# Head loop of a hybrid GDN, S5 and cross-attention block in a new order: unnormalized q and k, earlier convolutions, masks first on Pool, transposes in the triangular inverse

## Chip, cores and metric

One core of one Trainium2 chip. The metric is device time in microseconds, the median of the runs; lower is better. TensorE does the matmuls, VectorE the elementwise work, ACT the activations, Pool (GpSimd) elementwise work and some transfers, SP the weight loads.

## The reference, cut to what matters

One layer on x of 512 x 2048 in float32. x is normalized and multiplied by w_in; the columns of the product feed three branches and their gates. The branch of this case is the gated delta rule, 8 heads of 128:

```python
qkv = jax.nn.silu(causal_depthwise_conv(qkv_raw, conv_w))
q = l2norm(q) * (GDN_HEAD_DIM ** -0.5)
k = l2norm(k)
...
lower = jnp.where(strict, jnp.einsum('bnhid,bnhjd->bnhij', k_beta, k) * decay, 0.0)
sol = lax.linalg.triangular_solve(eye + lower, rhs, left_side=True, lower=True, unit_diagonal=True)
...
v_new = u_n - jnp.einsum('bhcd,bhde->bhce', w_n, state)
o = jnp.einsum('bhcd,bhde->bhce', qd_n, state) + jnp.einsum('bhij,bhje->bhie', qk_n, v_new)
...
o = rmsnorm(o, out_norm_g)
```

l2norm divides by the root of a row's sum of squares plus 1e-6, rmsnorm by the root of the mean of squares plus 1e-6. A second branch, S5, is a complex linear recurrence in groups; a third is attention to a memory. At the end the gated branches are multiplied by their weights, summed and multiplied by w_out.

## The kernel before, in words

The program runs in phases that all engines leave together: set-up, attention, the head loop (mixer), the S5 gate product, the branch products and the output product. Large products are made of float32 numbers split in a high part of reduced precision (ACT, `split_hi`, L402) and the rest (VectorE, `split_lo`, L411), with three matmuls of 512 columns for each tile (`mm3`, L420). Two weight buffers alternate: a block's load into raw waits until TensorE has used the block two before (`load_halves`, L370).

**The head loop.** In a trip (`mixer`) TensorE computes ten blocks of 128 columns of the input projection for head a: q, k, v, a gate, z_b, a gate, z_a, two gates, x_b. Each block is eight eighths of six matmuls, so a trip has 80 eighths. Between them stands the small work of two older heads: j = a - 1 goes through norms, decays, the triangular inverse and the S5 inputs, l = a - 2 through its recurrence over four chunks of 128, its output norm and the store. `until(e)` on TensorE issues big matmuls up to eighth e; what stands after it runs next. An eighth waits for its half of the block's wl, and the first one also until ACT has emptied the PSUM bank. The order of every engine is written by hand, and each works strictly in order; semaphores are waited for where a value or a buffer is needed. Ten trips are run, mixers 0 to 9: 0 has blocks only, 1 has no l, 2 to 8 are full, 9 has l and two blocks.

**The order of before.** On VectorE (`mixer`, L1706), split(b) makes the low half of block b + 1. After split(0) come the states of the recurrence, the three convolutions of j (`convolve`, L1577) and the S5 matrices; after split(1) the S5 states of group 0 (`s5_states`, L1678: six products from PSUM, then two scans) and the gated output of l (`gated`, L1669: reciprocal, gain, z); after split(2) the decays' differences and the scaling of k and q (L1603, L1609); after split(3) `keys`, `system`, `values`; then the first level of the inverse (`first_level`, L1639) and six levels (`level_x`, `level_p`). `keys` (L1619) writes kbg, and kbg also holds the gated output of l until it is stored: the wait on g_st at L1625 is for that store, which Pool issues in `store_head` (L612).

On ACT (`mixer`, L1287), end_of(b) empties block b (`tile_out`) and splits block b + 2. The split of block 1 stands first, then the negated weights (`weights_out`), new values, SiLU and squares of q, k and v, the S5 tables (`s5_tables`, sine and cosine) and roots.

On Pool (`mixer`, L553) stand the arguments of the S5 tables for group 0, the S5 store, arguments(1), turn_back(0) (the S5 states turned back by the tables), the head's store, the masks (strict and upper triangle, times beta), and the rest.

**The inverse.** It is built by doubling: tl holds it, tu its transpose. A level multiplies the transposed lower matrix by tl (`level_x`, L843), VectorE masks the product to gx, and TensorE forms two products, tu with gx for the change of tl and gx with tu for that of tu (`level_p`, L855, L861 and L862). A float32 product of 128 columns is two passes in the profile; a transpose is one.

## Time and profile before

| | us |
|---|---|
| median of 3 runs | 2438.35 |
| lowest, highest | 2429.41, 2440.11 |
| profiled execution, its own time | 2434.2 |
| its span | 2432.6 |
| VectorE busy | 1272.6 |
| ACT busy | 816.4 |
| Pool busy | 718.8 |

The span runs from the first to the last instruction of the profiled execution. A busy share is a mean over stages that have different limits. Matmul rows overlap, so the distance between two starts tells what one costs, not its duration.

### The profile page before, as it was taken

What the parts mean: (1) busy time and instruction counts of PE and PEld (TensorE: products, weight loads), DVE (VectorE), ACT (ScalarE), POOL (GpSimd) and SP (SyncE); (2) the same over time, 40 slices, a digit from 0 to 9 for tenths busy, and PEclk for the clock granted to TensorE, in tenths of its full rate; (3) what the DMA queues carried; (4) which work ended last, traced back from release to release, by engine and by line L of the source; (5) the groups of instructions that cost most, each with busy time, mean ns of one, the idle gap of its engine ahead of it and who ended that gap; (6) DMA issues with size and microseconds to landing.
All of it is one profiled execution on the core that took longest, in us unless ns stands there. A gap on an engine that the chain in (4) does not pass through costs nothing.

```text
span 2432.6 us, 29926 instructions
## 1 busy us (share of the span) xinstructions
PE 2292.5 (94%) x10744; PEld 1816.8 (75%) x10744; DVE 1272.6 (52%) x1495; ACT 816.4 (34%) x1042; POOL 718.8 (30%) x554
## 2 busy tenths in 40 slices
PE   4999999999999999999999999999999989999996
PEld 3888876877767777677777776776777877877885
DVE  4433332286495584864955848648523334445233
ACT  5433321353252432422524324325224222123221
POOL 0000000066284372642843726627310100000000
PEclk9999998999999999999999999999999999999998
DMA  4444432422322222222322322232235545554343
GB/s 159 122 122 121 115 101 70 122 79 75 87 80 81 65 81 75 69 78 80 83 76 72 82 75 69 78 84 80 77 91 160 174 137 166 156 162 147 115 129 111
DMA packets 374343, 249.74 MB, mean 103 GB/s; under 512 B 21305, under 2 KB 349186, under 8 KB 372738
## 3 DMA queue, kind: packets, MB, share of 16 engines
q1 hardware_dynamic: 355954, 193.21, 29.1%
q0 software_dynamic: 11408, 43.00, 5.3%
q10 hardware_dynamic: 6912, 12.59, 1.4%
q8 instruction: 47, 0.77, 0.1%
q14 instruction: 22, 0.18, 0.0%
HBM read 221.50 MB, written 27.26 MB: 102 GB/s over the span
## 4 chain that ended last, share of the span: by engine, by line
PE 79%; DVE 9%; DMA 5%; ACT 4%; issue 2%; SPq 0%; DVEq 0%; POOLq 0%; ACTq 0%; POOL 0%
PE bank L422 22%; PE bank L424 22%; PE bank L423 21%; DMA raw<-in_w_in_dram 4%; DVE wl L416 2%; PE bank L862 2%; PE bank L861 2%; PE bank L852 2%; PE bank L919 1%; PE bank L926 1%; ACT wh L408 1%; PE bank L927 1%; PE bank L920 1%; DVE rk L1605 1%; DVE tl L1671 1%
## 5 line engine op out<-in xcount | busy, mean ns | idle before, releaser
L416 DVE TENSOR_TENSOR wl<-raw,wh 128x1024 fp32r<-128x1024 f32 x352 | 474.5, 1359 | 605.6 <-ACT wh L408 605.1
L422 PE MATMUL bank<-uh,wh 128*128 128x512 f32 (+1 forms) x1808 | 747.6, 414 | 15.7 <-DVE wl L416 10.9
L423 PE MATMUL bank<-ul,wh 128*128 128x512 f32 (+1 forms) x1808 | 709.1, 392 | 0.0
L424 PE MATMUL bank<-uh,wl 128*128 128x512 f32 x1792 | 706.2, 394 | 0.0
L408 ACT ACTIVATE wh<-raw 128x1024 fp32r<-128x1024 f32 x352 | 370.5, 1057 | 700.5 <-DMA raw<-in_w_in_dram 306.2
L422 PEld LDWEIGHTS bank<-uh,wh 128*128 128x128 f32 (+1 forms) x1808 | 341.4, 189 | 139.6 <-issue 61.6
L424 PEld LDWEIGHTS bank<-uh,wl 128*128 128x128 f32 x1792 | 339.0, 189 | 75.7
L423 PEld LDWEIGHTS bank<-ul,wh 128*128 128x128 f32 (+1 forms) x1808 | 341.9, 189 | 69.5 <-issue 6.5
L422 PE MATMUL bank<-gh,wh 128*128 128x512 f32 x512 | 202.6, 396 | 12.2 <-DVE gl L1774 12.2
L424 PE MATMUL bank<-gh,wl 128*128 128x512 f32 x512 | 200.9, 392 | 0.0
L423 PE MATMUL bank<-gl,wh 128*128 128x512 f32 x512 | 200.2, 391 | 0.0
L565 POOL TENSOR_SCALAR karg<-cst,s5h 128x512 f32<-128x512 f32 x32 | 39.7, 1241 | 346.8 <-DVE hph L1555 219.4
L1206 ACT ACTIVATE gk<-bank 128x512 f32<-128x512 f32 x48 | 28.7, 597 | 277.6 <-PE bank L424 277.4
L422 PEld LDWEIGHTS bank<-gh,wh 128*128 128x128 f32 x512 | 96.7, 189 | 33.4 <-issue 11.4
L585 POOL TENSOR_TENSOR hr<-tcos,gr 128x512 f32<-128x512 f32 x32 | 48.6, 1520 | 247.2 <-PE bank L927 189.6
L542 POOL DMA_DIRECT2D gated_c<-ox x8 | 4.5, 565 | 369.9 <-DVE ox L1466 369.4
L424 PEld LDWEIGHTS bank<-gh,wl 128*128 128x128 f32 x512 | 96.5, 189 | 22.4
L423 PEld LDWEIGHTS bank<-gl,wh 128*128 128x128 f32 x512 | 96.7, 189 | 21.0
L422 PE MATMUL bank<-wh,uh 128*128 128x512 f32 x256 | 100.2, 391 | 3.2 <-DVE ul L1803 3.2
L424 PE MATMUL bank<-wh,ul 128*128 128x512 f32 x256 | 100.3, 392 | 0.0
L423 PE MATMUL bank<-wl,uh 128*128 128x512 f32 x256 | 100.3, 392 | 0.0
L672 POOL DMA_DIRECT2D gates<-gates x24 | 17.1, 713 | 237.0 <-DVE merged L1791 148.1
(301 smaller groups left out, 3257.6 us busy)
## 6 DMA issues: line engine op xcount, KB each, us to landing
raw<-in_w_in_dram SPq DMA_DIRECT2D x224, 512.0 KB, 3.9
raw<-in_w_kv_mem_dram SPq DMA_DIRECT2D x32, 512.0 KB, 3.9
raw<-in_w_out_dram SPq DMA_DIRECT2D x32, 512.0 KB, 3.9
gates<-gk ACTq DMA_DIRECT2D x48, 256.0 KB, 4.4
gates<-gates POOLq DMA_DIRECT2D x24, 512.0 KB, 4.6
raw<-in_s_w_glu_dram SPq DMA_DIRECT2D x16, 512.0 KB, 3.8
raw<-in_w_br_c_dram SPq DMA_DIRECT2D x16, 512.0 KB, 3.8
raw<-in_w_br_a_dram SPq DMA_DIRECT2D x16, 512.0 KB, 3.8
```

Source lines behind the costliest of these rows:

```text
L408: act.activation(k.wh[slot][:, c], k.raw[slot][:, c], ACT.Copy).then_inc(k.w_hi, 1)
L416: dve.tensor_tensor(k.wl[slot][:, c], k.raw[slot][:, c], k.wh[slot][:, c].bitcast(F32), ALU.subtract).then_inc(k.w_lo, 1)
L422: pe.matmul(o, ah, bh, start=start, stop=False)
L423: pe.matmul(o, ah, bl, start=False, stop=False)
L424: return pe.matmul(o, al, bh, start=False, stop=stop)
L565: ts(k.karg[:, :], k.tvec, hi_, ROUND, ALU.mult, ALU.add).then_inc(k.args, 1)
L585: pool.tensor_tensor(o[:, :], c1[:, :], a[:, :], ALU.mult).then_inc(k.dem, 1)
L852: mm = pe.matmul(ps[2][:, n * P:(n + 1) * P], k.lt[:, n, :], k.tl[:, n, :], start=True, stop=True)
L861: pe.matmul(ps[6][:, c], k.tu[:, n, :], k.gx[:, n, :], start=True, stop=True)
L862: mm = pe.matmul(ps[7][:, c], k.gx[:, n, :], k.tu[:, n, :], start=True, stop=True)
L919: pe.matmul(ps[3][:, :], k.bc[r, 0, :], k.xb[r, :], start=True, stop=True)
L1206: act.activation(k.gk[n][:, :], o[:, :], ACT.Sigmoid).then_inc(k.mx_out, 1)
```

## The change

The keys and queries are not normalized any more. The squares of k are summed in columns (`norm_keys`: the squares as weights, one column of ones), which gives one number for each row; its reciprocal, times beta and decays, is folded into small tiles (`key_scales`, hk) that scale the masks, kbg and the values. The query's norm is folded into the output norm: the squares of q, scaled by the constant of the norm, are added to the sum of squares of the output in the same bank. The convolutions and SiLU of head a are done in the trip that projects them, near its end. On Pool the masks and decayed queries come before the head's store and before arguments(1). In levels 1 to 5 the second product goes; tl is updated first and its transpose, by four TensorE transposes, is copied to tu. `level_x` now waits for tl alone. The weights product of l comes before the trip's first eighth, the S5 output of group 3 right after it, and most small work of j stands at other eighths. ACT does the negated weights before the split of block 1, and the S5 tables of group 1 before end_of(2). The functions left out below have only their waits and scale tiles changed to match.

```diff
-        if j: arguments(1); turn_back(0)
+        if j: masks(); decayed_queries()
         if l: store_head()
-        if j: masks(); arguments(2); decayed_queries(); turn_back(1); arguments(3); turn_back(2); turn_back(3)
+        if j: arguments(1); turn_back(0); arguments(2); turn_back(1); arguments(3); turn_back(2); turn_back(3)
...
     def norm_keys(j):
-        pe.wait_ge(k.sq, count(j, 2, 2))
-        wait(pe, k.oroot, count(j, 0, 1))
-        pe.matmul(ps[6][:, :], ones, k.rk[:, :], start=True, stop=True).then_inc(k.ss, 1)
+        pe.wait_ge(k.sq, count(j, 1, 2))
+        for n in range(NT):
+            mm = pe.matmul(ps[6][:, n:n + 1], k.rk[:, n * P:(n + 1) * P], ones[:, 0:1], start=True, stop=True)
+        mm.then_inc(k.ss, 1)
         pe.wait_ge(k.gu, count(j, 1, 1))
         wait(pe, k.st_s, count(j, 0, 3))
         pe.matmul(ps[7][:, :], ones, k.gx[:, :, :], start=True, stop=True).then_inc(k.rsum, 1)
...
     def keys(j):
-        pe.wait_ge(k.qk, count(j, 1, 2))
+        pe.wait_ge(k.silu, count(j, 2, 3))
+        pe.wait_ge(k.rn, count(j, 1, 4))
+        wait(pe, k.oroot, count(j, 0, 1))
...
+    def level_t(j, l):
+        pe.wait_ge(k.tus, count(j, 2 * l - 1, 11))
+        for n in range(NT):
+            mm = pe.transpose(ps[7][:, n * P:(n + 1) * P], k.tl[:, n, :], ident)
+        mm.then_inc(k.ltt, 1)
...
-    def output_norm(j):
+    def output_norm(j, nxt):
         pe.wait_ge(k.osq, count(j, 1, 1))
-        pe.matmul(ps[6][:, :], ones, k.lt[:, :, :], start=True, stop=True).then_inc(k.sso, 1)
+        pe.wait_ge(k.sq, count(j, 2, 2))
+        if nxt:
+            pe.wait_ge(k.rn, count(nxt, 1, 4))
+        pe.matmul(ps[6][:, :], ones, k.lt[:, :, :], start=True, stop=False)
+        pe.matmul(ps[6][:, :], ones, k.rq[:, :], start=False, stop=True).then_inc(k.sso, 1)
...
+        if l: weights(l)
         until(1)
-        if l: weights(l)
+        if l: s5_outputs(l, 3)
...
         if l: chunk_output(l, 3)
-        until(11)
-        if l: output_norm(l)
+        until(10)
+        if j: norm_keys(j)
         until(13)
+        if l: output_norm(l, j)
+        until(15)
         if j: s5_matrices(j)
-        until(15)
+        until(18)
         if j: s5_inputs(j, 0)
-        until(17)
-        if j: norm_keys(j)
-        until(25)
-        if j: norm_queries(j)
+        until(20)
+        if j: keys(j)
+        until(21)
+        if j: keys_keys(j)
+        until(26)
+        if j: values(j)
         until(29)
-        if j: keys(j); keys_keys(j); s5_inputs(j, 1)
+        if j: turn_lower(j)
         until(31)
-        if j: values(j); s5_outputs(j, 0)
+        if j: keys_queries(j)
         until(33)
-        if j: turn_lower(j)
+        if j: s5_inputs(j, 1)
         until(36)
-        if j: keys_queries(j)
+        if j: s5_outputs(j, 0)
+        until(38)
+        if j: level_x(j, 1)
+        until(41)
+        if j: level_p(j, 1)
+        until(43)
+        if j: level_t(j, 1)
         until(45)
-        if j: level_x(j, 1); s5_inputs(j, 2)
+        if j: level_x(j, 2); s5_inputs(j, 2)
         until(48)
-        if j: level_p(j, 1)
-        until(51)
-        if j: level_x(j, 2)
+        if j: level_p(j, 2)
+        until(50)
+        if j: level_t(j, 2)
         until(52)
-        if j: s5_outputs(j, 1)
-        until(54)
-        if j: level_p(j, 2)
+        if j: level_x(j, 3); s5_outputs(j, 1)
+        until(55)
+        if j: level_p(j, 3)
         until(57)
-        if j: level_x(j, 3)
+        if j: level_t(j, 3)
+        until(58)
+        if j: level_x(j, 4)
         until(60)
-        if j: level_p(j, 3); s5_inputs(j, 3)
+        if j: s5_inputs(j, 3)
+        until(61)
+        if j: level_p(j, 4)
         until(63)
-        if j: level_x(j, 4)
-        until(66)
-        if j: level_p(j, 4)
+        if j: level_t(j, 4)
+        until(65)
+        if j: level_x(j, 5)
         until(67)
         if j: s5_outputs(j, 2)
         until(69)
-        if j: level_x(j, 5)
-        until(72)
         if j: level_p(j, 5)
-        until(75)
+        until(71)
+        if j: level_t(j, 5)
+        until(74)
         if j: level_x(j, 6)
-        until(78)
+        until(77)
...
+        if l: weights_out(l)
         split_hi(k, act, B_MIX + 1, PER, a)
-        if l: weights_out(l); new_values(l, 0); new_values(l, 1); new_values(l, 2)
+        if l: new_values(l, 0); new_values(l, 1)
         if j: tile_out(j, M_XB)
-        if l: new_values(l, 3)
-        if j: activation_of(j, 0)
+        if l: new_values(l, 2); new_values(l, 3); output_squares(l)
         end_of(0)
-        if l: output_squares(l)
-        if j: s5_matrices(j); activation_of(j, 1); activation_of(j, 2); s5_tables(j, 0)
+        if j: row_decays(j); decays(j)
         if l: output_root(l)
+        if j: key_root(j); s5_matrices(j); s5_tables(j, 0); query_squares(j)
         end_of(1)
-        if j: key_root(j); s5_tables(j, 1)
         if blocks > 2:
+            if j: s5_tables(j, 1)
             end_of(2)
-            if j: query_root(j); decays(j); keep_z(j)
+            if j: keep_z(j); lower_turned(j)
             end_of(3)
-            if j: lower_turned(j)
             end_of(4)
             if j: s5_tables(j, 2)
             end_of(5)
             end_of(6)
             if j: s5_tables(j, 3)
             end_of(7)
+            if gate is None: activation_of(a, 0)
             end_of(8)
+            if gate is None: activation_of(a, 1); activation_of(a, 2); key_squares(a)
...
+    def key_scales(j):
+        dve.wait_ge(k.ss, count(j, 1, 1))
+        ts(k.hk[:, 0, :], ps[6][:, 0:NT], EPS, None, ALU.add).then_inc(k.rn, 1)
+        dve.wait_ge(k.rn, count(j, 1, 4))
+        dve.reciprocal(k.hk[:, 0, :], k.hk[:, 0, :]).then_inc(k.rn, 1)
+        dve.wait_ge(k.rn, count(j, 2, 4))
+        tt(k.hk[:, 1, :], k.hk[:, 0, :], k.hph[:, 2, :], ALU.mult).then_inc(k.rn, 1)
+        tt(k.hk[:, 2, :], k.hk[:, 0, :], k.hph[:, 0, :], ALU.mult).then_inc(k.rn, 1)
...
         wait(dve, k.g_st, count(j, 0, 16))
-        tt(k.kbg[:, :, :], chunked(ps[6][:, :]), rows(k.hph[:, 2, :]), ALU.mult).then_inc(k.kb, 1)
+        dve.wait_ge(k.rn, count(j, 3, 4))
+        tt(k.kbg[:, :, :], chunked(ps[6][:, :]), rows(k.hk[:, 1, :]), ALU.mult).then_inc(k.kb, 1)
...
+    def level_t(j, l):
+        dve.wait_ge(k.ltt, count(j, l, 5))
+        dve.tensor_copy(k.tu[:, :, :], chunked(ps[7][:, :])).then_inc(k.tus, 1)
...
         split(0)
         if l: state(l, 0)
         if j: head_parameters(j)
-        if l: state(l, 1); s5_sum(l)
+        if l: s5_sum(l)
         if j: log_decays(j)
+        if l: state(l, 1)
         if l: state(l, 2)
-        if j: convolve(j, 0); s5_matrices(j); convolve(j, 1); convolve(j, 2)
+        if j: s5_matrices(j); key_scales(j); differences(j)
         split(1)
         if j: s5_states(j, 0, 0); s5_states(j, 0, 1)
         if l: gated(l)
+        if j: keys(j); system(j)
         split(2)
-        if j: differences(j); normed_keys(j)
-        if j: normed_queries(j)
+        if j: values(j); first_level(j); queries(j)
         split(3)
-        if j: keys(j); system(j); values(j); s5_states(j, 1, 0); s5_states(j, 1, 1)
+        if j: s5_states(j, 1, 0); s5_states(j, 1, 1)
         split(4)
-        if j: first_level(j); queries(j)
+        if j: level_x(j, 1); level_p(j, 1); level_t(j, 1)
+        if j: s5_states(j, 2, 0)
         split(5)
-        if j: level_x(j, 1); s5_states(j, 2, 0); level_p(j, 1)
+        if j: level_x(j, 2); s5_states(j, 2, 1); level_p(j, 2); level_t(j, 2)
+        if heads: conv_weights(a); convolve(a, 0)
         split(6)
-        if j: s5_states(j, 2, 1); level_x(j, 2); level_p(j, 2)
+        if j: level_x(j, 3); level_p(j, 3); level_t(j, 3); level_x(j, 4)
         split(7)
-        if j: level_x(j, 3); level_p(j, 3); s5_states(j, 3, 0); level_x(j, 4); s5_states(j, 3, 1)
+        if j: s5_states(j, 3, 0); level_p(j, 4); s5_states(j, 3, 1); level_t(j, 4)
+        if heads: convolve(a, 1)
         split(8)
-        if j: level_p(j, 4); level_x(j, 5); level_p(j, 5)
+        if j: level_x(j, 5)
+        if heads: convolve(a, 2)
+        if j: level_p(j, 5); level_t(j, 5)
         split(9)
         if j: level_x(j, 6); level_p(j, 6)
```

## Rows read from the trace of the kernel before

**Rows 1.** The page: span, then TensorE's busy time, share of span and instructions.
```profile
span 2432.6 us, 29926 instructions
...
PE 2292.5 (94%) x10744; PEld 1816.8 (75%) x10744; DVE 1272.6 (52%) x1495; ACT 816.4 (34%) x1042; POOL 718.8 (30%) x554
```

**Rows 2.** Windows: trips (mixers 1 and 5), then 3.4 us; PEclk is granted clock.
```profile
489.40:636.30 146.90, 146.07 (x683) 113.35 (x682) 105.97 (x115) 55.46 (x66) 84.89 (x57) 1.00 0.31 82
...
1124.67:1287.50 162.83, 156.63 (x731) 119.82 (x730) 107.77 (x122) 57.94 (x73) 85.71 (x59) 0.99 0.28 76
...
1130.60:1134.00 3.40, 3.40 (x10) 2.82 (x11) 0.64 (x1) 0.28 (x1) 0.00 (x0) 0.50 0.00 0
```

**Rows 3.** Waits of TensorE: who waited for whom, us in total, times, longest.
```profile
PE bank L880 <- ACT dl L1272: 17.7, 8, 3.3
...
PE bank L901 <- ACT lt L1280: 11.7, 8, 3.3
...
PE bank L817 <- DVE kc L1607: 9.9, 7, 2.2
...
PE bank L861 <- DVE gx L1653: 6.8, 8, 2.5
```

**Rows 4.** Timeline of TensorE in one trip: start, us, what, idle before.
```profile
1163.71 1.02 PE L798 MATMUL bank<-rk,cst 128*128 128x512 f32 x2
1164.56 1.02 PE L801 MATMUL bank<-gx,cst 128*128 128x512 f32 x2
...
1173.40 0.39 PE L424 MATMUL bank<-uh,wl 128*128 128x512 f32 x1
...
1174.76 0.39 PE L424 MATMUL bank<-uh,wl 128*128 128x512 f32 x1
1176.44 0.50 PE L422 MATMUL bank<-uh,wh 128*128 128x512 f32 x1 [1.30 <-DVE wl L416]
...
1197.08 0.60 PE L840 MATMUL bank<-cst,dl 128*128 128x128 f32 x4
1197.43 0.48 PE L422 MATMUL bank<-uh,wh 128*128 128x512 f32 x1
...
1222.18 0.38 PE L861 MATMUL bank<-gx,tu 128*128 128x128 f32 x2
...
1223.88 0.48 PE L422 MATMUL bank<-uh,wh 128*128 128x512 f32 x1
```

**Rows 5.** Timeline of VectorE in the same trip.
```profile
1130.01 1.23 DVE L416 TENSOR_TENSOR wl<-raw,wh 128x1024 fp32r<-128x1024 f32 x1 [5.11 <-ACT wh L408]
...
1161.15 0.69 DVE L1692 TENSOR_TENSOR ma<-bank,tcos 128x512 f32<-128x512 f32 x1 [3.35 <-PE bank L920]
...
1165.25 2.19 DVE L1699 TENSOR_TENSOR_SCAN gr<-s5h,gr 128x512 f32<-128x512 f32 x1
...
1168.93 3.32 DVE L1671 RECIPROCAL tl<-lt 128x512 f32<-128x512 f32 x1
...
1174.08 4.54 DVE L416 TENSOR_TENSOR wl<-raw,wh 128x1024 fp32r<-128x1024 f32 x2
...
1192.23 0.68 DVE L1626 TENSOR_TENSOR kbg<-bank,hph 128x512 f32<-128x512 f32 x1
...
1194.03 0.68 DVE L1617 TENSOR_TENSOR vb<-bank,hph 128x512 f32<-128x512 f32 x1
...
1209.04 1.78 DVE L1645 TENSOR_TENSOR tu<-lt,cst 128x512 f32<-128x512 f32 x1
...
1231.27 1.22 DVE L1699 TENSOR_TENSOR_SCAN gr<-s5h,gr 128x512 f32<-128x512 f32 x1
...
1233.53 0.67 DVE L1653 TENSOR_TENSOR gx<-bank,cst 128x512 f32<-128x512 f32 x1
```

**Rows 6.** Timeline of Pool, its store; then the transfer's size and us to landing.
```profile
1182.07 0.62 POOL L614 DMA_DIRECT2D gated_a<-kbg  x1 [0.83 <-POOL hi L588]
...
gated_a<-kbg POOLq DMA_DIRECT2D x1, 256.0 KB, 2.4
```

More of the change, by code:

```diff
@@ L51 @@
 C_COL = C_T + S
-COLS = ["eps", "eps128", "quarter", "even", "odd", "neven", "nodd"]
+COLS = ["eps", "epssq", "quarter", "even", "odd", "neven", "nodd"]
 NCONST = C_COL + len(COLS)
@@ L561, in arguments @@
             if q == 0:
-                wait_apart(k, pool, k.sliced, count(j, 3, 3))
+                wait_apart(k, pool, k.sliced, count(j, 2, 2))
             wait_apart(k, pool, k.tab, count(j, 3 * q, 12))
@@ L801, in norm_keys @@
         pe.matmul(ps[7][:, :], ones, k.gx[:, :, :], start=True, stop=True).then_inc(k.rsum, 1)
-    def norm_queries(j):
-        wait(pe, k.og, count(j, 0, 2))
-        pe.matmul(ps[2][:, :], ones, k.rq[:, :], start=True, stop=True).then_inc(k.ss, 1)
     def values(j):
         pe.wait_ge(k.silu, count(j, 3, 3))
-        pe.wait_ge(k.root, count(j, 2, 2))
+        wait(pe, k.og, count(j, 0, 2))
         for n in range(NT):
@@ L828, in keys_queries @@
     def keys_queries(j):
-        pe.wait_ge(k.qk, count(j, 2, 2))
+        pe.wait_ge(k.silu, count(j, 1, 3))
         pe.wait_ge(k.vb_s, count(j, 1, 1))
@@ L857, in level_p @@
         pe.wait_ge(k.xm, count(j, l, 6))
+        if l == 1:
+            pe.wait_ge(k.tu_s, count(j, 4, 4))
+        else:
+            pe.wait_ge(k.tus, count(j, 2 * (l - 1), 11))
         for n in range(NT):
@@ L860, in level_p @@
             if l < 6:
[L861 to L862 removed]
+                mm = pe.matmul(ps[6][:, c], k.tu[:, n, :], k.gx[:, n, :], start=True, stop=True)
+            else:
+                mm = pe.matmul(ps[7][:, c], k.gx[:, n, :], k.tu[:, n, :], start=True, stop=True)
         mm.then_inc(k.lp, 1)
+    def level_t(j, l):
[3 more added lines that the diff above has]
+        mm.then_inc(k.ltt, 1)
     def weights(j):
@@ L1583, in convolve @@
         wait(dve, k.vtr, count(j, 0, 1))
+        wait(dve, k.sq, count(j, 0, 2))
+        wait(dve, k.pm, count(j, 0, 4))
         ts(dst[:, :], src[:, 0:S], k.cwh[:, 0, part:part + 1], None, ALU.mult).then_inc(k.conv, 1)
```

80 lines of the change are left out of this document (41 added, 39 removed).

## The prediction

> **What bounds the kernel now.** I read the page first. TensorE works in 94% of the span [rows 1], so time comes off in two ways only: fewer matrix passes, or shorter holes between them. VectorE, at 52%, matters where TensorE stands waiting for it. The profiled execution took 2434.2 us, 1.6 more than its span; the median of the three runs is 4 us higher. The windows by trip come second: a full trip of the head loop takes 162.8 us, of which TensorE is idle 6.2 [rows 2]. Seven trips are full (blocks, head work and recurrence together, mixers 2 to 8); the one before has head work but no recurrence, the last has recurrence alone. Third, the waits of TensorE name the holes [rows 3]: 17.7 us in 8 trips at the first new value, 11.7 at the output norm, 9.9 at the transposes of k, 6.8 at a level. A sixth hole, 1.3 us, stands before block 3 in one timeline [rows 4]. After the hole at the new values TensorE runs 3.4 us at a granted clock of 0.50, which is 1.2 GHz instead of 2.4 [rows 2].
>
> I count time as eighths of a block. Six matmuls of 512 columns lie between 1173.40 and 1174.76, so an eighth is 1.36 us [rows 4]. From that and the passes between them I can say when TensorE comes to each block, and from VectorE's timeline when that block's low half is ready.
>
> **What the change takes away, per full trip.**
> - The negated weights no longer stand behind a split that waits for its transfer: 17.7/8 = 2.2 us, and most of the slow clock behind it (3.4 us at half speed is 1.7; I take 1.2, as not every trip need have it).
> - Squares of the output right behind the last value: 11.7/8 = 1.5. k isn't scaled any more: 9.9/7 = 1.4. The level's hole: 0.9. The old hole before block 3: 1.3.
> - Passes. A level's two products take 1.70 us from 1222.18 to 1223.88 [rows 4], so one takes 0.85. Its replacement, four transposes, is a row of 0.60 including the tail of its pipeline [rows 4]; 0.45 with the step back to the big matmuls. That is 0.4 saved, five times: 2.0. The k norm took 0.85 (1163.71 to 1164.56 [rows 4]); eight passes of one column are not in the trace and cost between nothing and 0.85 (the eight of a level product); I take 0.45, saving 0.4. The q norm only moves into the output norm: 0. Both reciprocals of 512 columns and two products leave VectorE, with no gain by themselves; the convolutions move to the end of the trip, where VectorE has waits of several us between levels, also 0, and if that cover were gone they'd cost 3 us each. One ACT table switch more or less lies beside TensorE: 0.
>
> Together 8.5 + 2.4 = 10.9 us.
>
> **What it adds.** Here I walk VectorE's queue, because it is strictly in order.
>
> Block 3. VectorE's list was: S5 states of group 0, gated output, split of block 3, and keys much later. It becomes: states, gated output, *keys, system*, split of block 3. `keys` overwrites kbg, which the gated output has just filled and Pool stores to memory, so L1625 waits for that store to land. Before, some 18 us lay between; now nothing does. From the start of the states: products 4.1 (1161.15 to 1165.25), the two scans 3.7 with Pool at work or, as Pool will then be idle, 2.3 (1231.27 to 1233.53), reciprocal and gating 5.15 less 0.35 for the same reason [rows 5]; Pool's wake-up and issue 0.7 and 2.4 to landing [rows 6]; three products at 0.6 (1192.23 to 1194.03), so 1.8; first half of the split 2.3 (half of 4.54) as Pool has started its arguments again, or 1.2 if it does not collide [rows 5]. Sum 18.4, or 17.3. TensorE's side: before, from 1161.15 to the end of the big matmul that starts 1174.76 are 13.8 us [rows 4, 5]: nine eighths and the norm. Now the S5 inputs come at eighth 18 instead of 15, so six eighths, 8.2, and the twelve passes of keys and k-by-k at 0.106 each, 1.3, less the start-up of 0.1: 9.4. TensorE stands **9.0 us** (7.9 without the collision). Behind a hole of 2.2 on average it fell to half clock [rows 2, 3], so I add 1.5. Behind the waiting keys in VectorE's queue stand the split, the values and the first level.
>
> Block 4. The split of block 4 now stands behind `first_level` and `queries`. From the transposes of the lower matrix: copy 0.8, three VectorE operations of 1.78 (L1645) [rows 5], queries 0.6, first half of the split 2.3 = 8.8. TensorE has three eighths and the eight k-by-q passes, 5.0. Hole **3.8**. The 1.78 are with Pool busy, and Pool, whose arguments and turn-back of group 0 were all pushed behind the store, is busy then. Were it idle they'd take about 0.62 (half of 1.23 for 1024 columns) and the split 1.2: no hole. So 0 to 3.8; I take 3.8, the nearest rows being the same operations. ACT's copy of that matrix now stands behind the tables of group 1, and these behind Pool's arguments, later by the store; I find it ready about when the transposes are, and count nothing.
>
> Level 2. The S5 inputs of group 2 come at eighth 45, level 2's second product at 48, three eighths = 4.1 later. VectorE needs 0.3 + 2.05 (three products), the whole split of block 6 (4.54, or 2.46 alone) and the mask 0.7: 7.6 or 5.5. Hole 1.4 to 3.5, taken 3.3 (arguments of group 3 run beside it). Then VectorE does the second part of the states, 2.05 + 2.3, and 0.7 for the difference, before the transposes can go: 5.2 against 3.6 of TensorE: **1.6**. A second fall of the clock behind these, half likely: 0.8.
>
> From there to the end of the trip I find every split ready at least 1 us early, the last level by 0.6 only.
>
> Added: 9.0 + 1.5 + 3.8 + 3.3 + 1.6 + 0.8 = 20.0. Net **+9.1 per full trip, +64** for seven. The trip without recurrence has no store and no gating: block 3 costs only 1, so 1 + 3.8 + 3.3 + 1.6 + 0.8 - 3.2 (0.8 of its holes and the 2.4 of passes) = +7. The last trip gains its two holes and clock and pays two more passes: -4. With the profiled 2434.2 that is 2501; I say **2500**, and as the median stands 4 above that execution the error from this is small.
>
> **A rule that speaks against the transposes.** In the trace the four transposes of L840 are followed by big matmuls at the usual pace, and the clock does not fall there [rows 2, 4]. The Trainium skill, TensorE: Matmul & The Clock Gate, Part 4 (PE-mode transpose), says that transposes do not count as TensorE activity for the clock gate the way products do. By it five more such groups per trip could let the clock fall; the trace does not bear this out for four passes between long products.
>
> **Rivals.**
> - *Clock falls at the transposes.* Five groups, up to 1.7 us each: 8.5 a trip, 68 in all: 2568. Against it the row of L840. 3%.
> - *The holes close* (the other side). The store's landing, the collisions and the level order don't reach TensorE, because VectorE comes to its splits earlier than I walk. All of the 10.9 stays: 2434 - 76 - 3 - 4 = 2351. It decides where the new holes together fall under 10.9 us a trip. For it: VectorE loses 8 us of work a trip. Against it: block 3's 7.9 alone needs no collision. 9%, with its milder forms 12%.
> - *Even.* Pool and VectorE never collide and the clock stays up: 7.9 + 0 + 0 + 1.4 + 1.6 = 10.9 against 10.9: about 2434, with one clock fall 2445. The walk's errors of a microsecond a trip put it either side. 12%.
> - *The tail too.* With Pool's work later, the last level (0.6 us early) and the convolutions before it come late as well, 2 to 3 us a trip: 2518. 15%, inside the range.
> - *The change does not do what it says*: the masks are first on Pool but wait for the decays, which need TensorE's sum at eighth 10, so Pool idles in front of them; that is in my walk and needs no case.
>
> **Numbers.** My case (net +4 to +13 a trip, 2460 to 2530) has 58%, the tail 15%, the clock rival 3%, even 12%, holes closed 12%. About 0.5% (12 us) can be told from no change: the even case gives 11 of its 12 to the middle and one to faster, so faster 0.13, same 0.11, slower 0.76. The range goes from the even case, 2430, to all costs high (the store landing 2 us later, a third fall of the clock: +14 a trip), 2535.
>
> **What would show it.** Right: TensorE's longest waits are for the split wl, about 9 us once a trip before block 3, VectorE idle 3 us before kbg on a transfer named gated, then 3 to 4 us before block 4; granted clock under 1 behind them; no wait left at the new values; about 2.4 us less TensorE work per trip. Wrong: if VectorE's wait before kbg is under 1 us, the term of the store falls; if TensorE arrives at block 3 later than 47 us into the trip, my count of passes is off; if the wait before block 4 is missing, the collision was.

## The result, and the profile after

The kernel after takes **2499.43 us** (median of 4 runs, 2498.14 to 2501.73); the kernel before took 2438.90 in the runs beside it. The ratio is **1.0268**, 95% interval 1.0246 to 1.0290: slower by 60.5 us. The forecast was 2500. One execution of the nine of experiment 4 took 4625.43 us and stands in no ratio.

The page of the profiled execution after, the span and the line of busy times:

```profile
span 2499.7 us, 29937 instructions
...
PE 2306.1 (92%) x10632; PEld 1815.2 (73%) x10632; DVE 1177.0 (47%) x1503; ACT 801.4 (32%) x1032; POOL 701.2 (28%) x554
```

Beside [rows 1] VectorE has 96 us less to do, ACT 15 and Pool 18, and TensorE issues 112 matmuls fewer. Yet TensorE's busy time is 14 us *longer*, and the span 67: fewer passes took more time, which points to the clock; the rest of the 67 is holes, less what the passes gave back.

Windows of the kernel after: the trips of mixers 1 and 3, then 3.4 us behind its first hole (us; busy time of PE, PEld, DVE, ACT, POOL; granted clock, DMA share, GB/s):

```profile
489.30:640.90 151.60, 145.08 (x676) 111.20 (x674) 90.74 (x115) 52.99 (x64) 83.23 (x57) 1.00 0.30 79
815.56:988.60 173.04, 159.67 (x719) 120.15 (x718) 95.18 (x122) 56.37 (x72) 81.65 (x59) 0.94 0.27 72
870.00:873.40 3.40, 3.39 (x8) 2.72 (x9) 2.24 (x2) 0.00 (x0) 3.19 (x2) 0.50 0.00 0
```

A full trip took 162.8 us with a granted clock of 0.99 [rows 2]; now it takes 173.0 with 0.94. The seven full trips are 169.6 to 176.2 us long, together 60.5 us more than before, and mixer 1 is 4.7 longer.

TensorE's waits, and two of VectorE's, in the kernel after (total us, times, longest):

```profile
PE bank L425 <- DVE wl L419: 77.8, 16, 8.7
DVE tu L1694 <- ACT lt L1309: 32.7, 8, 5.0
DVE kbg L1675 <- DMA gated_a<-kbg: 22.0, 7, 3.4
PE bank L869 <- DVE gx L1702: 17.4, 8, 2.7
PE bank L878 <- DVE tl L1707: 13.3, 13, 2.1
```

All four lines of [rows 3] are gone. In their place TensorE waits for the low half of a block's weights (wl), in 7 trips twice, and at levels 2 and 5 of the inverse.

TensorE's timeline in one trip after (start, us, what, idle before):

```profile
835.37 0.95 PE L803 MATMUL bank<-cst,rk 128*128 128x1 f32 x8
836.18 1.10 PE L807 MATMUL bank<-gx,cst 128*128 128x512 f32 x2
...
870.01 0.79 PE L425 MATMUL bank<-uh,wh 128*128 128x512 f32 x1 [7.87 <-DVE wl L419]
...
887.52 0.50 PE L425 MATMUL bank<-uh,wh 128*128 128x512 f32 x1 [2.42 <-DVE wl L419]
...
925.33 1.15 PE L869 MATMUL bank<-gx,tu 128*128 128x128 f32 x8 [1.32 <-DVE gx L1702]
...
930.13 0.66 PE L878 MATMUL bank<-cst,tl 128*128 128x128 f32 x4 [0.91 <-DVE tl L1707]
930.54 0.47 PE L425 MATMUL bank<-uh,wh 128*128 128x512 f32 x1
```

VectorE's timeline in the same trip:

```profile
852.65 0.69 DVE L1746 TENSOR_TENSOR ma<-bank,tcos 128x512 f32<-128x512 f32 x1 [9.74 <-PE bank L940]
...
859.01 3.33 DVE L1725 RECIPROCAL tl<-lt 128x512 f32<-128x512 f32 x1
...
863.16 0.69 DVE L1730 TENSOR_TENSOR kbg<-kbg,zk 128x512 f32<-128x512 f32 x1
866.93 0.69 DVE L1675 TENSOR_TENSOR kbg<-bank,hk 128x512 f32<-128x512 f32 x1 [3.09 <-DMA gated_a<-kbg]
...
868.74 3.43 DVE L419 TENSOR_TENSOR wl<-raw,wh 128x1024 fp32r<-128x1024 f32 x2
...
881.40 0.95 DVE L1694 TENSOR_TENSOR tu<-lt,cst 128x512 f32<-128x512 f32 x1 [3.69 <-ACT lt L1309]
882.27 1.76 DVE L1696 TENSOR_TENSOR tl<-cst,tl 128x512 f32<-128x512 f32 x1
883.96 1.78 DVE L1698 TENSOR_TENSOR tu<-cst,tu 128x512 f32<-128x512 f32 x1
```

Read these two side by side and the chain of the first hole stands there: states, reciprocal, gating, the store (3.09 us of waiting in front of kbg), three products, half a split, TensorE. From 852.65 to 870.01 are 17.36 us. The prediction's walk gave 18.4, or 17.3 without the collision. Note also the first row: VectorE is **idle for 9.7 us in front of this chain**.

Pool and ACT in the same trip after, and the store's transfer (256 KB, us to landing):

```profile
864.51 0.58 POOL L619 DMA_DIRECT2D gated_a<-kbg  x1 [16.65 <-DVE kbg L1730]
...
875.27 0.62 POOL L579 TENSOR_SCALAR farg<-farg 128x512 f32<-128x512 f32 x1 [0.20 <-POOL farg L577]
```

```profile
876.07 0.63 ACT L1258 ACTIVATE tsin<-farg 128x512 f32<-128x512 f32 x1 [23.00 <-POOL farg L579]
...
880.78 0.59 ACT L1309 ACTIVATE lt<-bank 128x512 f32<-128x512 f32 x1
```

```profile
gated_a<-kbg POOLq DMA_DIRECT2D x8, 256.0 KB, 2.4
```

Here is a second chain, of which the prediction counted nothing: the same gated output, the store, Pool's seven operations of arguments(1) (to 875.9), ACT's tables, and only behind them ACT's copy of the lower matrix, which VectorE needs for the first level and, behind that, for the split of block 4.

**The account per full trip**, by adding up the idle stretches between TensorE's matmuls over the seven trips. What is lost to the clock is an estimate: half of TensorE's busy time at 1.2 GHz.

| us per trip | before | after | predicted after |
|---|---|---|---|
| hole at block 3 | 1.3 | 8.0 | 9.0 |
| hole at block 4 | 0 | 2.3 | 3.8 |
| level 2, product and transposes | 0 | 2.2 + 0.8 | 3.3 + 1.6 |
| level 5, transposes | 0 | 0.7 | 0 |
| other holes | 5.9 | 0.1 | 0 |
| lost to the clock | 1.7 | 6.1 | 2.8 |

Holes +6.8, clock +4.4 (before rounding 4.35); the trips grew by 60.5/7 = 8.6, so the passes gave 2.5 back (predicted 2.4). (The 2.8 is 2.3 added and the 0.5 that the prediction left of the old 1.7.)

### The profile page after: what moved, and what is told of

Same layout as the page of the kernel before. It is cut to its first block and busy times, and to the rows that moved or that the text cites. A ratio compares the mean times of both kernels' runs of the same rounds, so it can differ in the third digit from the quotient of the medians.

```text
span 2499.7 us, 29937 instructions
## 1 busy us (share of the span) xinstructions
PE 2306.1 (92%) x10632; PEld 1815.2 (73%) x10632; DVE 1177.0 (47%) x1503; ACT 801.4 (32%) x1032; POOL 701.2 (28%) x554
## 5 line engine op out<-in xcount | busy, mean ns | idle before, releaser
L425 PE MATMUL bank<-uh,wh 128*128 128x512 f32 (+1 forms) x1808 | 762.0, 421 | 82.7 <-DVE wl L419 77.8
L419 DVE TENSOR_TENSOR wl<-raw,wh 128x1024 fp32r<-128x1024 f32 x352 | 448.0, 1288 | 598.4 <-ACT wh L411 597.3
L426 PE MATMUL bank<-ul,wh 128*128 128x512 f32 (+1 forms) x1808 | 718.5, 397 | 0.0
L427 PE MATMUL bank<-uh,wl 128*128 128x512 f32 x1792 | 715.0, 399 | 0.0
L425 PEld LDWEIGHTS bank<-uh,wh 128*128 128x128 f32 (+1 forms) x1808 | 346.9, 192 | 211.0 <-DVE wl L419 74.3
L427 PEld LDWEIGHTS bank<-uh,wl 128*128 128x128 f32 x1792 | 344.3, 192 | 79.0
L426 PEld LDWEIGHTS bank<-ul,wh 128*128 128x128 f32 (+1 forms) x1808 | 347.9, 192 | 67.1 <-issue 4.5
L1746 DVE TENSOR_TENSOR ma<-bank,tcos 128x512 f32<-128x512 f32 x64 | 44.1, 689 | 158.0 <-PE bank L940 142.5
L426 PEld LDWEIGHTS bank<-gl,wh 128*128 128x128 f32 x512 | 97.2, 190 | 21.5
L568 POOL TENSOR_SCALAR karg<-cst,s5h 128x512 f32<-128x512 f32 x32 | 24.6, 768 | 237.7 <-DVE hph L1596 202.4
```

The source lines that it names most:

```text
L419: dve.tensor_tensor(k.wl[slot][:, c], k.raw[slot][:, c], k.wh[slot][:, c].bitcast(F32), ALU.subtract).then_inc(k.w_lo, 1)
L425: pe.matmul(o, ah, bh, start=start, stop=False)
L426: pe.matmul(o, ah, bl, start=False, stop=False)
L427: return pe.matmul(o, al, bh, start=False, stop=stop)
L568: ts(k.karg[:, :], k.tvec, hi_, ROUND, ALU.mult, ALU.add).then_inc(k.args, 1)
L1746: tt(k.ma[:, :], x1[:, :], c[:, :], ALU.mult).then_inc(k.mod, 1)
```

## The experiments

Unless said otherwise each is the kernel after with one edit. But for 7, 8 and 10 TensorE's order stays that of the kernel after, so holes can be compared by place. Where ranges per trip are given without more, they are those of mixers 2 to 7.

**1. The split in front of the whole chain.**

```diff
         split(1)
+        split(2)
         if j: s5_states(j, 0, 0); s5_states(j, 0, 1)
         if l: gated(l)
         if j: keys(j); system(j)
-        split(2)
```

> The changed kernel with one move on VectorE: the split of block 3 stands before the S5 states of group 0 and the gated output, instead of behind keys and system. The hole of 7.9 us before block 3 must go in every theory. Theory A (one chain: gated output, store, Pool's arguments of group 1, ACT's tables of group 1, copy of the lower matrix, first level, split of block 4): the split pushes that whole chain 2 to 3 us later, so block 4 begins at 74 to 75 us of the trip instead of 72.0; the hole before block 4 grows from 2.3 to some 14 us and the time is 2500 to 2520. Rival B (the hole before block 3 is a cost of its own): 7.9 us and up to 3 us of slow clock come off each of seven trips, the hole before block 4 stays near 2.3, and the time is 2425 to 2445.

Measured 2506.88 us, ratio 1.0299 (1.0264 to 1.0333): A, with a smaller hole than its 14. The hole at block 3 is gone in every trip; one of 11.2 us stands before block 4 (10.1 in mixer 8), one of 0.9 before the values. The clock loses 1.5 to 5.8 in mixers 2 to 7, in stretches of up to 20.5 us. Two waits of this kernel:

```profile
PE bank L425 <- DVE wl L419: 83.1, 9, 11.2
DVE tu L1694 <- ACT lt L1309: 69.5, 8, 10.9
```

So the hole is no property of block 3: it is a debt that the next block pays. The second line says what it waits for: VectorE stands 8.7 us a trip before the first level, until ACT's copy is there; in the kernel after it was 4.1.

**2. The store from a tile of its own**, so that nothing waits for its landing before the last level.

```diff
-                           k.kbg[:, :, :].rearrange("p n c -> p (n c)")).then_inc(k.g_st, 16)
+                           k.gout[:, :, :].rearrange("p n c -> p (n c)")).then_inc(k.g_st, 16)
...
-        wait(dve, k.g_st, count(j, 0, 16))
...
         tt(k.kbg[:, :, :], chunked(ps[6][:, :]), rows(k.hk[:, 1, :]), ALU.mult).then_inc(k.kb, 1)
...
-        stt(k.kbg[:, :, :], chunked(ps[2][:, :]), k.prm2[:, 104:105], k.tl[:, :, :], ALU.mult, ALU.mult)
+        stt(k.gout[:, :, :], chunked(ps[2][:, :]), k.prm2[:, 104:105], k.tl[:, :, :], ALU.mult, ALU.mult)
...
-        if j: level_x(j, 6); level_p(j, 6)
+        if j: wait(dve, k.g_st, count(j, 0, 16)); level_x(j, 6); level_p(j, 6)
```

> The changed kernel with a buffer of its own for the gated output, so that keys does not wait for the store. In both theories the wait before kbg (3.1 us) goes and the hole before block 3 falls from 7.9 to 4.8 us. Theory A: Pool issues the store and its arguments at the same moment as before, so block 4 still begins at 71 to 72 us of the trip and its hole grows to about 5; time 2490 to 2500. Rival B (the store wait costs what it takes): 3.1 us in each of seven trips and a little slow clock, 2470 to 2478.

Measured 2512.57, ratio 1.0308 (1.0275 to 1.0341). A's mechanism, above both ranges: the hole at block 3 falls by the 3.1 us of the store to 4.85, the one at block 4 grows from 2.3 to between 5.0 and 6.7 in mixers 2 to 7, and the clock loses 3.5 to 11.7 a trip. The holes' sum hardly changed (13.6 for 14.0); the time went up. Its window of a trip (mixer 4):

```profile
995.00:1170.90 175.90, 162.44 (x719) 122.55 (x718) 94.37 (x122) 56.37 (x72) 79.51 (x59) 0.93 0.26 71
```

**3. Pool's arguments in front of the store.**

```diff
-        if j: masks(); decayed_queries()
+        if j: masks(); decayed_queries(); arguments(1)
         if l: store_head()
-        if j: arguments(1); turn_back(0); arguments(2); turn_back(1); arguments(3); turn_back(2); turn_back(3)
+        if j: turn_back(0); arguments(2); turn_back(1); arguments(3); turn_back(2); turn_back(3)
```

> The changed kernel with Pool's arguments of group 1 before the store of the head, in the 16 us in which Pool waits for the gated output. Theory A says the Pool part of the chain goes, but the transposes of the lower matrix, which wait for keys, are ready at nearly the same moment (80.1 against 80.8 on one clock), so alone it brings little: hole before block 3 stays 7.9, the copy of the lower matrix comes 0.5 us earlier, time 2485 to 2500. Rival C (Pool's late arguments are the main fault): block 4's hole and the later ones close, 2455 to 2475.

Measured 2472.67, ratio 1.0147 (1.0116 to 1.0178): in C's range, well under A's. The hole at block 3 stays (8.4; 9.1 in mixer 8), that at block 4 falls to 0.5 in most trips (1.5 at most), and the clock loses 2.4 to 3.6 in the full trips. C's "and the later ones close" isn't borne out: those at levels 2 and 5 stay, 1.3 to 2.6, 0.9 and 0.8. VectorE at the first level in this kernel, and Pool beside it:

```profile
876.49 0.69 DVE L1694 TENSOR_TENSOR tu<-lt,cst 128x512 f32<-128x512 f32 x1 [4.03 <-ACT lt L1309]
877.10 0.69 DVE L1696 TENSOR_TENSOR tl<-cst,tl 128x512 f32<-128x512 f32 x1
877.70 1.77 DVE L1698 TENSOR_TENSOR tu<-cst,tu 128x512 f32<-128x512 f32 x1
```

```profile
875.70 1.57 POOL L575 TENSOR_SCALAR karg<-cst,s5h 128x512 f32<-128x512 f32 x1 [0.21 <-POOL farg L573]
877.45 1.47 POOL L577 TENSOR_TENSOR farg<-farg,karg 128x512 f32<-128x512 f32 x1 [0.18 <-POOL karg L575]
```

Two of the three take 0.69 instead of 0.95 and 1.76. Pool isn't idle beside them, it is at arguments(2); what changed is the kind of its operation. The two that are quick begin beside a TENSOR_SCALAR, the slow third beside a TENSOR_TENSOR, and in the kernel after all three stand beside TENSOR_TENSORs of turn_back(0) (880.50 to 885.18). ACT's copy waits for TensorE's transposes (97.2 us in 8 trips) and no longer for Pool.

**4. All repairs that I then believed in, together**: 2 and 3, the split of block 3 before the gated output, that of block 4 before the values, ACT's tables(1) behind end_of(2), level 2 reordered, and the last convolution behind level 5; that of q stayed in front of level 3.

> All together: own buffer for the gated output, Pool's arguments before the store, the split of block 3 before the gated output, the split of block 4 before the values, ACT's end of block 2 before the tables of group 1, the split of block 6 and the mask of level 2 before the S5 states of group 2, the last convolution behind level 5. Theory A: with the chain cut at each link TensorE has under 1 us of holes in a trip and no slow clock, a trip takes 151 to 153 us, and the whole 2350 to 2370, well under the kernel before (2439). Rival B adds up the single terms and comes to the same here, so it is the three others that tell them apart. If the passes saved are less than I counted (2.4 us a trip), the trip stays at 154 and the time at 2375.

Measured 2449.43, ratio 1.0067 (1.0050 to 1.0084): 80 us above the range, a miss. Waits and VectorE's timeline of this kernel:

```profile
PE bank L870 <- DVE gx L1701: 44.2, 7, 6.4
...
PE bank L814 <- DVE gout L1729: 21.9, 7, 3.2
```

```profile
1081.33 5.05 DVE L1634 SCALAR_TENSOR_TENSOR qc<-qraw,cwh,qc 128x512 f32<-128x512 f32 x3
1086.30 4.48 DVE L420 TENSOR_TENSOR wl<-raw,wh 128x1024 fp32r<-128x1024 f32 x2
1090.70 0.68 DVE L1701 TENSOR_TENSOR gx<-bank,cst 128x512 f32<-128x512 f32 x1
```

Two new holes with one cause each. The values' bank is free only once the gated output has been read from it, and that now stood behind a split: 3.2 us. And in front of gx of level 3 stood a convolution (5.05, where the same three took 2.33 in a trip of the kernel after) and a split of 4.48: 6.4 us. In mixer 8, which has no next head to convolve, the 6.4 is missing and the trip takes 158.4 instead of 167.3. So both orders have to be walked to the end of the trip.

**5. One line moved: the gated output in front of the states**, into VectorE's 9.7 idle us.

```diff
         split(1)
+        if l: gated(l)
         if j: s5_states(j, 0, 0); s5_states(j, 0, 1)
-        if l: gated(l)
         if j: keys(j); system(j)
```

> The changed kernel with one move on VectorE: the gated output of l stands before the S5 states of group 0, in the 9.7 us in which VectorE waits for the S5 products. Theory A (one chain through the gated output and its store): reciprocal and gating fit in that wait, the store is out by 34 us of the trip and keys finds it landed, Pool's arguments follow at once. The first half of the split of block 3 ends at 46.6 to 47.8 us against 46.3 wanted: hole 0.5 to 1.5 instead of 7.9, little slow clock; block 4 keeps a hole of 1 to 4 us since first level and queries still stand before its split. Trip 158 to 162 us, time 2400 to 2435. Rival B (sum of the single terms: only the store's 3 us and the 5 of the gating leave): the same hole but all that follows unchanged, 2440 to 2450.

Measured **2398.65**, ratio 0.9843 (0.9817 to 0.9868), just under A's range. VectorE in this kernel:

```profile
985.60 3.35 DVE L1725 RECIPROCAL tl<-lt 128x512 f32<-128x512 f32 x1 [0.98 <-ACT lt L1325]
...
989.78 0.69 DVE L1730 TENSOR_TENSOR kbg<-kbg,zk 128x512 f32<-128x512 f32 x1
994.37 0.69 DVE L1746 TENSOR_TENSOR ma<-bank,tcos 128x512 f32<-128x512 f32 x1 [3.90 <-PE bank L940]
...
1001.04 0.66 DVE L1675 TENSOR_TENSOR kbg<-bank,hk 128x512 f32<-128x512 f32 x1
```

The reciprocal and gating fill the idle time, the store lands under the states, kbg waits for nothing. Holes at block 3 and 4 are 0.3 and 0.5 (1.3 and 0.6 in mixer 8), trips 157.9 to 158.9 us, and the clock loses at most 1.7. The holes of level 2 (2.5, and 0.9 in most) and level 5 (0.8) stay. Both chains begin at this one operation, so one move shortens both.

**6. That, and the rest of the chains cut**: split of block 3 before keys, of block 4 before the first level, ACT's tables(1) behind end_of(2), the mask of level 2 before the states of group 2, convolutions behind the levels that TensorE waits for.

```diff
-        if j: keys(j); system(j)
         split(2)
-        if j: values(j); first_level(j); queries(j)
+        if j: keys(j); system(j); values(j)
         split(3)
+        if j: first_level(j); queries(j)
...
-        if j: s5_states(j, 2, 0)
...
-        if j: level_x(j, 2); s5_states(j, 2, 1); level_p(j, 2); level_t(j, 2)
-        if heads: conv_weights(a); convolve(a, 0)
+        if j: level_x(j, 2); s5_states(j, 2, 0); level_p(j, 2); s5_states(j, 2, 1); level_t(j, 2)
         split(6)
-        if j: level_x(j, 3); level_p(j, 3); level_t(j, 3); level_x(j, 4)
+        if j: level_x(j, 3)
+        if heads: conv_weights(a); convolve(a, 0)
+        if j: level_p(j, 3); level_t(j, 3); level_x(j, 4)
...
```

> The kernel of the run before with the other links cut: the split of block 3 before keys, the split of block 4 before the first level, ACT's end of block 2 before the tables of group 1, the split of block 6 and the mask of level 2 before the S5 states of group 2, the second part of these behind level 2's difference, the convolution of q behind the mask of level 3 and that of v behind level 5. Theory A: no hole over 1 us in a full trip, no slow clock, trip 151 to 153.5, time 2350 to 2372. If a queue has again a hidden wait, one hole of 2 to 6 us shows at one place in every trip and the time is 2375 to 2430.

Measured **2345.48**, ratio 0.9628 (0.9603 to 0.9652): the fastest kernel here, 90.5 us under before in the runs beside it (2435.99), and under A's range by 5. A trip of it:

```profile
936.30:1087.90 151.60, 151.60 (x719) 116.53 (x718) 99.91 (x122) 56.64 (x72) 84.69 (x59) 1.00 0.30 82
```

TensorE's busy time equals the window: no hole in any full trip but one of 0.4, the clock never under 1.00. So 151.6 is what the passes cost by themselves. Mixers 2 to 7 of before took 162.6 in the mean; less 6.5 of holes, 1.1 of clock and 2.4 of passes that is 152.6. The kernel after gives the same, 152.4, without its holes and clock, so the last 0.8 goes with the holes as well (TensorE's start behind each would do it; this wasn't measured by itself).

**7. The same with two products per level**, as before, in place of product and transposes.

```diff
-                mm = pe.matmul(ps[6][:, c], k.tu[:, n, :], k.gx[:, n, :], start=True, stop=True)
-            else:
-                mm = pe.matmul(ps[7][:, c], k.gx[:, n, :], k.tu[:, n, :], start=True, stop=True)
+                pe.matmul(ps[6][:, c], k.tu[:, n, :], k.gx[:, n, :], start=True, stop=True)
+            mm = pe.matmul(ps[7][:, c], k.gx[:, n, :], k.tu[:, n, :], start=True, stop=True)
...
```

> The kernel of the run before with the two products of each level as in the kernel before, and without the transposes. By my count a level then costs TensorE 0.4 us more, 2.0 a trip, 16 us over eight trips: 16 to 18 us over the run before. Rival (the transposes lower the clock or cost a start-up of their own): difference 0 or below.

Measured 2366.36, ratio 0.9709 (0.9685 to 0.9733): 20.9 over experiment 6, 3 more than expected. A trip takes 3.2 us more, 0.9 of it a hole at the last level that wasn't expected; the other 2.3 are five levels at 0.46. The transposes give about what was predicted (0.4), and no full trip loses anything to the clock with them or without.

**8. The gain by itself**: the kernel before, with only ACT's negated weights moved in front of the split of block 1.

```diff
+        if l: weights_out(l)
         split_hi(k, act, B_MIX + 1, PER, a)
-        if l: weights_out(l); new_values(l, 0); new_values(l, 1); new_values(l, 2)
+        if l: new_values(l, 0); new_values(l, 1); new_values(l, 2)
```

> The kernel before with one move on ACT: the negated weights stand before the split of block 1. The hole at the first new value (2.1 us) and the slow clock behind it (1.7 us in five of seven trips, 2.9 in the last) must go: 8 holes of 2.2 and 11 us of clock, 28 us, so 2405 to 2415. Rival: the later split of block 1 opens a hole of its own before block 1, and the gain is under 10 us.

Measured 2410.84, ratio 0.9901 (0.9871 to 0.9931). The wait of [rows 3] at the new values is gone and with it the slow clock of mixers 2 to 7: trips 159.1 to 160.1, 3.0 us less in the mean. The prediction had 2.2 + 1.2. Mixer 8 gains nothing (171.8 for 171.4): its hole at the new values is gone, but it loses 8.1 to the clock where it lost 5.1.

**9. The split of block 3 in front of keys** (after the gated output).

```diff
-        if j: keys(j); system(j)
         split(2)
-        if j: values(j); first_level(j); queries(j)
+        if j: keys(j); system(j); values(j); first_level(j); queries(j)
```

> After, with one edit: the split of block 3 stands in front of keys and system in VectorE's queue, so it no longer waits for the store of the gated output. Theory A (the store wait is one half of a chain, and work pushed behind the split meets the next hole): the hole at block 3 falls from 7.9 to about 3.3 us (3.1 of wait and 1.8 of products no longer in front), but the keys, values and first level come later by the split's own time where the store has landed meanwhile, so the hole before block 4 stays at 2 to 3.5, and the clock behind the holes gives back some: trip 167 to 171, total 2462 to 2485. Theory B (the hole only moves, as when the split stood in front of the states): hole at block 4 over 6 us, total 2490 to 2510.

Measured 2503.90, ratio 1.0277 (1.0257 to 1.0298): B. The hole at block 3 falls to 2.9, but that before block 4 is 7.0 to 8.7. VectorE, then ACT, in this kernel:

```profile
1037.03 0.68 DVE L1692 TENSOR_TENSOR tl<-dl,cst 128x512 f32<-128x512 f32 x1
1048.43 1.66 DVE L1694 TENSOR_TENSOR tu<-lt,cst 128x512 f32<-128x512 f32 x1 [10.72 <-ACT lt L1309]
```

```profile
1043.12 0.63 ACT L1258 ACTIVATE tsin<-farg 128x512 f32<-128x512 f32 x1 [22.65 <-POOL farg L579]
...
1047.82 0.58 ACT L1309 ACTIVATE lt<-bank 128x512 f32<-128x512 f32 x1
```

VectorE idles 10.7 us in front of the first level. Theory A looked at VectorE's queue alone; in this kernel the hole is made by ACT's queue.

**10. The S5 inputs of group 0 two eighths sooner**: `until(18)` before them becomes `until(16)`.

> After, with one number changed: TensorE issues the S5 inputs of group 0 at eighth 16 instead of 18. VectorE stands idle 9.7 us in front of the states, so the whole chain (states, gating, store, keys, split, values, first level) starts 2.7 us sooner while TensorE's arrival at block 3 stays. Theory A (start of the states sets the block 3 hole): hole 7.9 falls to about 5.2, hole before block 4 unchanged as both sides of it shift with the hole, total 2470 to 2485 with some of the clock. Theory B (something else, the store's landing or Pool, sets it): block 3 hole within 1 us of 7.9, total 2492 to 2505.

Measured 2470.76, ratio 1.0133 (1.0114 to 1.0152): A's time with B's hole. The states start 2.2 us sooner (for the tables now, and not for TensorE), but block 3's hole shrinks only from 7.9 to 7.1; block 4's goes from 2.3 to 1.3 in the mean of the full trips, which neither theory had. VectorE and the store's transfer:

```profile
1012.07 0.69 DVE L1746 TENSOR_TENSOR ma<-bank,tcos 128x512 f32<-128x512 f32 x1 [7.50 <-ACT tcos L1261]
...
1027.81 0.69 DVE L1675 TENSOR_TENSOR kbg<-bank,hk 128x512 f32<-128x512 f32 x1 [4.54 <-DMA gated_a<-kbg]
```

```profile
gated_a<-kbg POOLq DMA_DIRECT2D x8, 256.0 KB, 3.7
```

The store now takes 3.7 us to land instead of 2.4, and eats 1.4 of the 2.2. Per full trip 1.6 us of holes and 2.5 of clock went, which for seven trips is the 29 us. The trace names what runs beside the store: in mixers 2 to 7 the next weight load (SP, 512 KB) begins 1.2 us after the store's issue, and 177 to 226 KB of it move between the store's first packet and its last; in the kernel after it was 7 KB at most. The store's first packet comes at 2.1 to 2.2 us instead of 1.2. Where the load begins later, in mixer 8 (2.0 us), the store lands in 2.6. No run moved the load alone.

**11. Experiment 9, and ACT's tables(1) behind the copy of the lower matrix.**

```diff
-            if j: s5_tables(j, 1)
             end_of(2)
-            if j: keep_z(j); lower_turned(j)
+            if j: keep_z(j); lower_turned(j); s5_tables(j, 1)
```

> The kernel with the split of block 3 before keys, and one more edit: ACT makes the S5 tables of group 1 behind its copy of the lower matrix instead of in front of it. Theory A (the hole that moved to block 4 is ACT's: store, Pool's arguments(1), 10.3 us, the tables, and only then the copy, 7.4 us after TensorE's transposes are done): the copy starts within 1 us of the transposes, VectorE's wait of 10.7 us for it falls to about 3, the hole before block 4 falls from 8.6 to between 0 and 3 (by whether its three operations take 0.68 or 1.7 with Pool busy), trip 163 to 167, total 2440 to 2462. Theory B (VectorE or Pool would be late anyway): hole at block 4 still over 5 us, total over 2485.

Measured 2469.31, ratio 1.0116 (1.0053 to 1.0180). In this kernel:

```profile
1033.81 1.35 DVE L1693 TENSOR_TENSOR tu<-lt,cst 128x512 f32<-128x512 f32 x1 [3.61 <-ACT lt L1309]
```

The hole before block 4 falls from 7.0 to 8.7 to between 2.1 and 3.2, VectorE's wait from 10.7 to 3.6, and 35 us of time go with it: the second chain runs through ACT's queue, and A's mechanism holds. The total is 7 us above A's range, as the clock took more and not less: 6.6 a full trip for 5.4, in spite of 5.6 us less of holes. One of the four executions took 2448.48, inside the range, the others 2468 to 2473.

**12. That edit alone, in the kernel after.**

> After, with that edit alone: the S5 tables of group 1 behind ACT's copy of the lower matrix. In after the copy starts 0.7 us behind the transposes, so both theories give little: A (the hole before block 4 is set in after by VectorE's three operations beside a busy Pool, and ACT is only the next in line): hole 2.3 falls to 1 to 2, trip shorter by 0.5 to 1.5 with some clock, total 2485 to 2497. B (ACT's queue sets this hole already in after): hole under 0.7, total 2465 to 2480.

Measured 2497.65, ratio 1.0252 (1.0212 to 1.0293): no difference from after that can be told. B is out; A's hole is 2.1 to 2.6 for its 1 to 2. In the kernel after ACT was only 0.7 us late, and three operations beside a busy Pool are what is left. In mixer 8 of this kernel Pool happens to be idle beside them, and there the hole is 0.9:

```profile
1748.97 0.69 DVE L1695 TENSOR_TENSOR tl<-cst,tl 128x512 f32<-128x512 f32 x1
1749.57 0.68 DVE L1697 TENSOR_TENSOR tu<-cst,tu 128x512 f32<-128x512 f32 x1
```

## Why the prediction was right

**The mechanism was right; that the sum came out so close is luck, a balance of two errors.** 9.1 us per trip were forecast and 8.6 came; mixer 1 cost 4.7 for 7. The last trip with the four blocks behind it gained 1 for 4: its own two blocks take 30.2 us for 37.5, but the blocks behind then wait 5.3 us for a split where they waited 1.5. The phases after that took 3.0 more in that one execution, of which the change moves nothing. Small slips in its sums cancel in part: the terms for block 4 add up to 9.0 and not 8.8, those behind level 2's mask to 5.05 and not 5.2, and level 2's upper value of 3.5 was taken as 3.3, together 0.3 us a trip.

**Block 3, 9.0, measured 8.0.** The walk's pieces hold singly: states 6.4 (4.1 + 2.3), reciprocal and gating 4.8, store 3.1, products 1.8, and TensorE's side 9.5 for 9.4. Only the choice between the two splits was wrong: its first half ended with TensorE's start at 870.01, 1.27 after 868.74, so it did not take the dearer value, and the other that the step gave, 7.9, is the one measured in six of seven trips. That the store is one link of the chain and not its cause is shown by 2 (its 3.1 us move to block 4) and by 5.

**Block 4, 3.8, measured 2.3.** In the trip shown the three operations took 4.3 instead of 5.3, the split's first half 1.3 instead of 2.3, ACT's copy came 0.7 late, and TensorE's side was 5.6 instead of 5.0. Right in kind: 3 and mixer 8 of 12 show the operations at 0.69 and the hole at 0.5 to 0.9, and 12 that they remain when ACT is out of the way. On this the Trainium skill, SBUF — State Buffer, section Who interferes with whom, says that VectorE's second port is shared with GpSimd under an exclusive lock; the trace agrees: with two tiles of SBUF as inputs 0.69 without Pool and up to 1.78 beside it, and with one input from a bank 0.69, also beside a TENSOR_TENSOR of Pool (ma at 919.89, Pool's L573 from 919.69 to 920.98). But "Pool busy", as the prediction has it, is too coarse: beside a TENSOR_SCALAR of Pool two of the three operations took 0.69 in 3.

**The step that failed without harm** is "I find it ready about when the transposes are, and count nothing" of ACT's copy. It was 0.7 us late in the kernel after, so the nothing was nearly right; but the row of the first chain hid a second one with almost the same length. Experiments 1, 2, 9 and 11 show it: shorten the first alone, or put the split in front of it, and 5 to 11 us appear at block 4; move the tables and they fall to 3. This is also why the rival "the holes close" was further away than it seemed from either side: neither the store nor the split alone could close them.

**Level 2, 3.3 + 1.6, measured 2.2 + 0.8.** In the trip shown the split in front of gx took 2.56 (922.03) and not 4.54, and the hole was 1.3; four of the seven trips had 2.6. I had taken the dearer value here too. **Level 5, 0, measured 0.7:** the convolution stands in front of the level there; "from there to the end every split ready" was true of the splits and missed the levels. Mixer 8 has no convolution and not this hole; 6 has neither.

**The clock, 2.8 left, measured 6.1: the largest error.** I took a fall to last as long as the one of [rows 2]. It lasted 3.4 to 10.2 us. I had one fall behind block 3 and half a one behind level 2; it also fell behind block 4 in six of seven trips, and behind level 2 in three. Its 3.3 us too little offset 3.7 too much in the holes.

**Passes, 2.4, measured 2.5.** By 7 a level gives 0.46 for 0.4. The eight one-column passes took 0.81 (835.37 to 836.18), the top of the range that I gave them, so the norm of k saved nothing for the 0.4 taken.

**The rivals.** The clock didn't fall at the transposes (6). The tail's mechanism came true in part, as 0.7 at level 5. "Even" had 7.9 at block 3 right and lacked block 4, half of level 2 and the clock. The change does what it says: Pool's masks end at 847.9, 17 us before the store.

**The gains** were right one by one: all holes of [rows 3] went, and by 8 the new values' alone is 3 us a trip. 6 shows what the change is worth where VectorE's order serves it.

## What to carry to other kernels

Follow a late operation on every queue that stands behind it, not only on the one where the hole appears: here one store released two chains, and shortening the first alone moved the hole one block on. Before making a chain shorter look for idle time in front of it: one line moved into 9.7 us of idle VectorE was worth 101 us, all the repairs of experiment 4 without it 50. And price a hole of TensorE with its clock: here holes of 2 us cost up to 1.7 more, and those of the kernel after, 2 to 8 us, 3 to 9 more a trip.

## What was not expected of the hardware

- **The clock added 4.4 us a trip to the holes' 6.8, and unevenly.** In experiment 12 mixers 2 to 7, with the same holes within 0.5 us, lost 3.2 to 7.2 us to it. Slow stretches lasted from 3.4 to 20.5 us. In the full trips of 5 and 6, with no hole over 2.6, the loss was 1.7 at most; but mixer 8 of 8, with none over 3.3, lost 8.1. What picks the length is open.
- **Transposes didn't bring it down.** In 6 five groups of four stand in each trip, and the granted clock is 1.00 in every full trip. The rule of the Trainium skill, TensorE: Matmul & The Clock Gate, Part 4 (PE-mode transpose), that they don't count as activity, costs nothing with four passes between long products.
- **Eight one-column passes (128x128 by 128x1) took 0.81 us**, as long as the eight of 128 columns at L837 (882.65 to 883.46 in the trip shown): columns are not what these small passes cost.
- **What VectorE pays beside Pool depends on Pool's operation.** In the fourteen traces a TENSOR_TENSOR of 128x512 with both inputs in SBUF took 0.70 at most with Pool idle throughout, up to 1.79 when it began beside a TENSOR_TENSOR of Pool, and 1.15 at most when it began beside a TENSOR_SCALAR and no TENSOR_TENSOR followed; with one input from a bank it never took over 0.70. Why the kinds differ wasn't tried.
- **A 256 KB store of Pool's queue landed in 3.7 us with a weight load beside it, and in 2.4 without** (10).
